# Attention stages with two sets of score banks, unnormalised probabilities and a shorter mask

## The reference

```
# windowed attention of the first block: 8 query heads, 2 key-value heads, head width 64
s_loc = where(|k_pos - q_pos| <= 128, q @ k.T / 8, -inf)      # keys of the tile and its two neighbours
s_ctx = q @ k_ctx.T / 8                                       # all 256 context keys
p = softmax(concat[s_loc, s_ctx, sink_of_head])[..., :-1]     # the sink is one more logit
o = p_loc @ v_loc + p_ctx @ v_ctx

# layers 0 and 1: all keys, no sink
grouped query:  o = softmax(q @ k.T / 8) @ v
differential:   o = (softmax(q1 @ k1.T / 8) - lambda * softmax(q2 @ k2.T / 8)) @ v   # v is 128 wide
```

## Time and profile before

| | |
|---|---|
| median of 3 runs | 4470.28 us (4470.28 to 4470.31) |
| profiled execution | 4471.72 us |
| its span, first to last instruction | 4469.9 us |
| TensorE busy | 3828.3 us |
| window attention | 388.2 to 494.4 us |
| attention of layer 0 | 1564.8 to 1775.9 us |
| attention of layer 1 | 3412.0 to 3579.9 us |

### The profile page before, as it was taken

How to read it: one execution, slowest core, us unless ns; L and a number is a source line. 1 busy time by engine, 2 the same in 40 slices (tenths; PEclk the granted TensorE clock), 3 DMA queues, 4 the chain that set the end, 5 groups by cost and what they waited for, 6 DMA issues and landing times. The chain is left out here.

```text
span 4469.9 us, 46232 instructions
## 1 busy us (share of the span) xinstructions
PE 3828.3 (86%) x18130; PEld 2589.8 (58%) x18130; DVE 1576.6 (35%) x2861; ACT 841.5 (19%) x1725; POOL 1002.0 (22%) x774
## 2 busy tenths in 40 slices
PE   6967967777589778999896999997896889888997
PEld 5865734444365355555453555554784657567886
DVE  3355320000221377334423322334116834334344
ACT  2123220000210155111112100001103511111001
POOL 1300200000023300123231322231142023334442
PEclk8978989899799989999998999998998999999999
DMA  4420289999511100122121223221120012121221
GB/s 187 186 76 15 86 312 396 396 393 400 195 38 57 38 1 1 64 84 87 67 96 38 81 108 113 101 80 46 38 74 16 1 60 82 62 80 60 89 88 48
DMA packets 79670, 496.35 MB, mean 111 GB/s; under 512 B 9568, under 2 KB 10976, under 8 KB 25696
## 3 DMA queue, kind: packets, MB, share of 16 engines
q1 hardware_dynamic: 69808, 469.80, 28.2%
q0 software_dynamic: 3792, 12.85, 0.9%
q10 hardware_dynamic: 5856, 10.75, 0.6%
HBM read 476.58 MB, written 16.78 MB: 110 GB/s over the span
## 5 line engine op out<-in xcount | busy, mean ns | idle before, releaser
L1679 PE MATMUL ps<-expert_weights,experts_x_turned 128*64 128x256 f32 x2112 | 286.3, 432 | 89.5 <-DMA expert_weights<-w_moe 88.0
L1679 PEld LDWEIGHTS ps<-expert_weights,experts_x_turned 128*64 128x64 f32 x2112 | 198.5, 156 | 186.2 <-issue 133.7
L550 PE MATMUL ps<-projected,weight_ring 128*128 128x384 f32 (+1 forms) x672 | 245.8, 521 | 0.0
L550 PEld LDWEIGHTS ps<-projected,weight_ring 128*128 128x128 f32 x672 | 127.7, 190 | 106.1 <-issue 45.9
L1762 DVE TENSOR_TENSOR experts_hidden<-experts_silu_gate,ps 128x256 f32<-128x256 f32 x33 | 13.9, 421 | 495.1 <-PE ps L1679 495.1
L2473 PE MATMUL ps<-h2b,weight_ring 128*128 128x384 f32 (+1 forms) x512 | 153.7, 444 | 23.7 <-PEq L237 23.7
L1977 PE MATMUL ps<-h2b,weight_ring 128*128 128x384 f32 (+1 forms) x512 | 155.1, 447 | 15.4 <-PEq L237 15.4
L814 PE MATMUL ps<-projected 64*128 64x256 f32 (+1 forms) x576 | 120.7, 536 | 54.6 <-ACT attention_prob L877 50.4
L2067 DVE SCALAR_TENSOR_TENSOR projected<-projected,sb_vectors 128x497 f32<-128x497 f32 (+26 forms) x270 | 157.8, 649 | 1.3
L2453 POOL TENSOR_TENSOR mlp_weight_sums<-weight_ring 128x512 f32<-128x512 f32 x32 | 43.6, 1363 | 469.9 <-DMA weight_ring<-w_stream 331.0
L1645 POOL DMA_INDIRECT experts_gathered<-tokens,own_tokens x32 | 28.9, 902 | 521.0 <-PE ps L1667 459.0
(11 more groups left out here) (666 smaller groups left out, 7549.1 us busy)
## 6 DMA issues: line engine op xcount, KB each, us to landing
weight_ring<-w_stream SPq DMA_DIRECT2D x218, 1024.0 KB, 5.0
expert_weights<-w_moe SPq DMA_DIRECT2D x198, 1024.0 KB, 27.6
slot_out<-experts_down_out ACTq DMA_DIRECT2D x66, 128.0 KB, 7.5
weight_ring<-w_stream SPq DMA_DIRECT2D x16, 512.0 KB, 3.7
weight_ring<-w_stream SPq DMA_DIRECT2D x16, 384.0 KB, 3.2
slot_out<-sb_constants SPq DMA_DIRECT2D x15, 256.0 KB, 5.1
sb_x_all<-xT SPq DMA_DIRECT2D x1, 3072.0 KB, 12.1
tokens<-h_tokens ACTq DMA_DIRECT2D x4, 512.0 KB, 4.9
```

What stands on the lines that cost most here:

```text
L550: ins = nc.tensor.matmul(core.ps[:, 2 * slot + half, 0:n], w_of(k), h_of(k)[:, a:a + n], start=(first and k == 0), stop=(last and k == chu ...
L1679: ins = nc.tensor.matmul(out[OWN * j:OWN * (j + 1), :], x_t[:, k, :], w[j][:, k, :], start=(k == 0), stop=(k == KD - 1), skip_group_check= ...
```

## The change

There are four edits.

**Score banks.** Even pairs use banks 0 to 2, odd pairs banks 3 to 5. The two heads lie one behind the other, 768 columns each, so the middle bank holds the end of head 0 and the beginning of head 1. Pieces are cut at bank boundaries: for 768 keys head 0 has 512 + 256 columns and head 1 has 256 + 512. Head 0's piece in the shared bank waits for head 1's. A peak starts when both heads' scores are done, an exponential when both peaks are. The turned probabilities use banks 6 and 7, and the output sum lies in the pair's first score bank, once exponential 0 of the next pair of that parity is done.

**Normalisation.** The exponentials are turned as they are. Their inverse sums are spread over 128 columns by GpSimd (`spread`), turned as one more tile behind the last turn, and copied out with it; VectorE multiplies the output by them when it takes it out of PSUM. For a differential pair VectorE first mixes map 1 into map 0 with the ratio -lambda * sum0 / sum1.

**Order.** The pipeline is one pair deeper: turns are those of p - 2, values those of p - 3, and the first of two turns goes ahead of the scores.

**Mask.** It is added on the two neighbour tiles alone, since the own tile is wholly allowed.

```
+        def scores(p, i):
+            flat = ps[:, 3 * (p % 2):3 * (p % 2) + 3, :].rearrange("p b n -> p (b n)")
+            return flat[:, i * T:(i + 1) * T]
+        flat_t = ps[:, 6:8, :].rearrange("p b n -> p (b n)")
+        def acc(p):
+            return ps[:, 3 * (p % 2), 0:P]
+        def factor(p):
+            b, keys = 2 * (p % 2) + sides[p] - 1, pairs[p]["keys"]
+            return prob_t[:, b, keys:keys + P]
...
             def score(p):
-                if p >= 1:
-                    pe.wait_ge(p_ready, 2 * p)
+                if p >= 2:
+                    pe.wait_ge(p_ready, 2 * p - 2)
+                if p >= 4:
+                    pe.wait_ge(o_out, p - 3)
+                cut = [pieces(i, pr["spans"]) for i in range(2)]
+                for j in range(max(map(len, cut))):
+                    for i in (0, 1) if j == 0 else (1, 0):
+                        if j < len(cut[i]):
+                            (q, k), (at, c, n) = pr["maps"][i], cut[i][j]
+                            if i == 0 and at >= 512:
+                                pe.wait_ge(shared_done, shares[p])
+                            ins = nc.tensor.matmul(scores(p, i)[:, at:at + n], q, k[:, c:c + n], start=True,
+                                                   stop=True, skip_group_check=True)
+                            if i == 1 and j == 0 and pr["keys"] > 512:
+                                ins.then_inc(shared_done, 1)
...
             def transpose(p, i):
-                pe.wait_ge(prob_ready, turn(p, i))
+                if pairs[p]["diff"]:
+                    pe.wait_ge(mixed, mixes[p])
+                else:
+                    pe.wait_ge(p_ready, 2 * p + i + 1)
...
+                if i == sides[p] - 1:
+                    pe.wait_ge(spread_ready, p + 1)
+                    ins = nc.tensor.transpose(flat_t[:, tiles * P:(tiles + 1) * P], spread[:, p % 2, :],
+                                              core.c("ident"))
...
             def values(p):
+                pe.wait_ge(p_ready, 2 * min(p + 2, N - 1) + 1)
...
-            for p in range(N + 2):
+            for p in range(N + 3):
+                if 0 <= p - 2 < N and sides[p - 2] == 2:
+                    transpose(p - 2, 0)
                 if p < N:
                     score(p)
-                if 0 <= p - 1 < N:
-                    transpose(p - 1, 0)
-                if p >= 2:
-                    values(p - 2)
-                if 0 <= p - 1 < N and sides[p - 1] == 2:
-                    transpose(p - 1, 1)
+                if 0 <= p - 2 < N:
+                    transpose(p - 2, sides[p - 2] - 1)
+                if p >= 3:
+                    values(p - 3)
...
         def _(act):
+                    exponential(p - 1, 0)
+                    copy_turned(p - 2, 0)
+                    exponential(p - 1, 1)
+                    copy_turned(p - 2, sides[p - 2] - 1)
...
+        @block.gpsimd
+                nc.gpsimd.tensor_tensor(
+                    spread[:, p % 2, :].rearrange("p (h n) -> p h n", h=n),
+                    core.ones[:, :].rearrange("p (h n) -> p h n", h=n),
+                    inv[:, b:b + n].unsqueeze(2).broadcast_to([P, n, P // n]), ALU.mult).then_inc(spread_ready, 1)
...
         def _(dve):
+            def inverse(p):
+                dve.wait_ge(p_ready, 2 * p + 2)
+                nc.vector.reciprocal(inv[:, b:b + 2], sums[:, b:b + 2]).then_inc(inv_ready, 1)
+                if pairs[p]["diff"]:
+                    nc.vector.tensor_scalar(ratio[:, r:r + 1], inv[:, b + 1:b + 2], sums[:, b:b + 1], neg_lambda,
+                                            ALU.mult, ALU.mult).then_inc(ratio_ready, 1)
+                    nc.vector.scalar_tensor_tensor(prob[:, b, 0:keys], prob[:, b + 1, 0:keys], ratio[:, r:r + 1],
+                                                   prob[:, b, 0:keys], ALU.mult, ALU.add).then_inc(mixed, 1)
+            def scale(p):
+                dve.wait_ge(o_done, turns[p])
+                nc.vector.tensor_tensor(pairs[p]["out"], acc(p), factor(p), ALU.mult).then_inc(o_out, 1)
...
+                    copy_turned(p - 2, 0)
+                    peak(p, 0)
+                    copy_turned(p - 2, 1)
+                    peak(p, 1)
+                    scale(p - 3)
+                    inverse(p - 1)
```

More of the change, by code:

```diff
@@ L753, in _, with attention_phase @@
             add(n - 1)
-def attention_phase(core, name, pairs, mask=None, neg_lambda=None):
+def attention_phase(core, name, pairs, masked=None, neg_lambda=None):
     nc, ps = core.nc, core.ps
-    masked = mask is not None
+    sink = 0 if masked is None else 1
     N = len(pairs)
@@ L766, in attention_phase @@
     turns = np.cumsum(sides).tolist()
-    wide = np.cumsum([n * (pr["keys"] > 512) for n, pr in zip(sides, pairs)]).tolist()
+    split = [not pr["diff"] and pr["keys"] > 512 for pr in pairs]
+    wide = np.cumsum([n * w for n, w in zip(sides, split)]).tolist()
+    shares = np.cumsum([pr["keys"] > 512 for pr in pairs]).tolist()
+    mixes = np.cumsum([pr["diff"] for pr in pairs]).tolist()
     with core.phase(name) as ph:
         prob = ph.sb("prob", [P, 4, T + 8])
-        prob_t = ph.sb("prob_t", [P, 4, T])
+        prob_t = ph.sb("prob_t", [P, 4, T + P])
         shift = ph.sb("shift", [P, 4])
@@ L773, in attention_phase, with turned @@
         inv = ph.sb("inverse", [P, 4])
[L774 to L777, removed]
[L778 to L783 removed]
+        ratio = ph.sb("ratio", [P, 2])
+        spread = ph.sb("spread", [P, 2, P])
+        s_done = [ph.sem(f"scores_done{i}") for i in range(2)]
+        shared_done, peak_ready, p_ready, inv_ready, ratio_ready, mixed, spread_ready, t_done, pt_act, pt_dve, o_done, \
+            o_out = [ph.sem(x) for x in (
+                "shared_bank_done", "peak_ready", "exp_done", "inverse_ready", "ratio_ready", "mixed", "spread_ready",
+                "turned", "pt_scalar", "pt_vector", "out_done", "out_scaled")]
+        block = ph.block()
+        def scores(p, i):
[7 more added lines that the diff above has]
+            return prob_t[:, b, keys:keys + P]
+        def turned(p, i):
+            return pairs[p]["keys"] + (P if i == sides[p] - 1 else 0)
         def turn(p, i):
@@ L789, in wides, with pieces @@
         def wides(p, i):
-            return wide[p] - (sides[p] - i - 1) * (pairs[p]["keys"] > 512)
+            return wide[p] - (sides[p] - i - 1) * split[p]
         def columns(p):
-            return pairs[p]["keys"] + masked
+            return pairs[p]["keys"] + sink
+        def pieces(i, spans):
+            out, at = [], 0
+            for c, n in spans:
+                while n:
+                    m = min(n, 512 - (i * T + at) % 512)
+                    out.append((at, c, m))
+                    at, c, n = at + m, c + m, n - m
+            return out
         @block.sync
@@ new lines, in score @@
+                if p >= 4:
[11 more added lines that the diff above has]
+                                ins.then_inc(shared_done, 1)
+                            if j == len(cut[i]) - 1 and not sink:
+                                ins.then_inc(s_done[i], 1)
@@ new lines, in score @@
+                if sink:
+                    for i in range(2):
+                        for at, c, n in pr["masked"]:
+                            nc.tensor.matmul(scores(p, i)[:, at:at + n], core.c("ident"),
+                                             masked[:, pr["tile"], c - NCTX:c - NCTX + n], start=False,
+                                             stop=True, skip_group_check=True)
+                        keys, row = pr["keys"], pr["sink"] + i
+                        nc.tensor.matmul(scores(p, i)[:, keys:keys + 1], core.ones[0:1, :],
+                                         core.row[0:1, row:row + 1], start=True, stop=True,
+                                         skip_group_check=True).then_inc(s_done[i], 1)
```

115 lines of the change are left out of this document (40 added, 75 removed).

## The result

The kernel after takes **4429.7 us** (median of 4 runs, 4428.44 to 4431.16), the kernel before 4470.3 in the same comparison: a ratio of 0.9909, 95% interval 0.9892 to 0.9926. The forecast was 4429.

What follows compares the result with a forecast made beforehand. TensorE was taken as busiest in attention (485 us), idle 1.11 us per differential pair awaiting exponentials. Gains 22.7 + 3.2 + 10.4 + 4 + 1 - 0.8, rounded to 41, from 4470.3 gave 4429 us, range 4416 to 4440.

Steps and rivals of the forecast that it cites:

- 64 pairs with 768 keys, steady: Attention of both layers: 32 differential pairs gain 0.71 us each (22.7), 32 grouped-query pairs 0.10 each (3.2).
- window stage: 16 window pairs: shorter mask 0.43 us each, fewer waits for exponentials, spread turn adds 0.11; net 0.65 each, 10.4.
- 16 pairs with 256 keys: Layer 0: full-clock period 2.92 to 2.3 us, but no better at 1.2 GHz; gain 0 to 12, taken as 4.
- filling and draining of the two layers: Pipeline ends, counted over three stages: deeper drain costs 4.5 us, freer filling gains 5.5 of 6.6; net 1.
- semaphores to clear: Four more semaphores per stage, cleared by GpSimd ahead of its next stage's first work: at most 0.8 us lost in all.
- I take 1.49 again: Scores of 768-key pairs: passes on both row halves still sum to 1.28 us, so the turn starts after 1.49, as before.
- neighbours end in order: Rival on the scores: a shorter matmul cannot end before a longer one issued ahead; 1.71 instead of 1.28 us, 4458; chance 0.17.
- Differential pairs: 768 keys: output multiply with hand-overs 0.38, scores 1.49, turn 0.82, values 1.50; period 4.19 us against 4.90.
- Grouped-query pairs: 768 keys, TensorE the bound: values 1.46, turn 0.85, scores 1.49, seven-tile turn 0.92; period 4.72 us against 4.82.
- The feared place: Grouped-query pairs: VectorE's copy between the peaks, called tightest; peak, copy, peak end at 4.6 us, values at 4.72.
- GpSimd and the seventh tile: Spread turn adds 0.11 us; GpSimd's multiply, bounded by 0.726, has up to 2 us of cover and costs nothing.
- the bounds that it names: Range of the main case, 4416 to 4440 us: clock 0 to 12, grouped pairs 0.02 to 0.14, filling 0 to 6.

Runs made afterwards that it cites:

- the first experiment: The changed kernel with head 1's 256-column score piece issued ahead of head 0's 512, the rest of the order kept: 4414.6 us, ratio to before 0.9874.

## Why the prediction was right in the sum, and where it was wrong

| term | predicted gain, us | measured, us |
|---|---|---|
| 64 pairs with 768 keys, steady | 22.7 + 3.2 | 8.1 |
| window stage | 10.4 | 11.2 |
| 16 pairs with 256 keys | 4 (0 to 12) | 10.4 |
| filling and draining of the two layers | 1, with the window's | 6.6, what is left of 36.3 |
| semaphores to clear; the rest of the program | -0.8 | 5.2, scatter |

**The step that failed: "I take 1.49 again".** The prediction let head 0's last piece start as soon as the array's half was free and head 1's 256 columns had passed. The half was free, and the columns had passed; the semaphore was not raised. The scores took 1.79 us to the turn instead of 1.49, 0.30 us in each of 64 pairs, 19 us, and the first experiment gave these back (19.1). The semaphore's own time is the missing number: 1.12 us after the group's start, with the piece itself done at 0.70. The rival "neighbours end in order" named the place, but had the mechanism half right and the price too high: by it head 1's 512 would have started 0.43 us late and the pass sum would have been 1.71, 27.5 us. Head 1's 512 started at 0.54, on time; only the piece behind the semaphore was late. By that rule of the Trainium skill (page "TensorE: Matmul & The Clock Gate", section Part 3: matmuls keep program order in start and in end) starts should keep the order too; here head 1's second pass of 256 starts at 0.33, ahead of head 0's second pass at 0.50, although head 0's matmul was issued first. Whether the end itself or only its signal keeps the order can't be told from the trace, since matmul ends are modelled in it. What a waiting engine sees keeps the order, and that is what the rule was worth here.

**Differential pairs.** Turn 0.82 and values 1.50 came as predicted. From the end of the values to the scores it took 0.48, not 0.38: the multiply is 0.29 as taken, but TensorE starts 0.15 us after its end (1643.51 + 0.29 = 1643.80; scores at 1643.95), where 0.05 had been counted. With the scores' 1.79 that makes 4.59. The first experiment's 4.29 is what the prediction's loop was worth without the semaphore; its remaining excess over 4.19 is this hand-over.

**Grouped-query pairs.** Turn of seven tiles 0.91 (taken as 0.92) and values 1.46 held; turn to scores was 0.80, taken as 0.85. With 1.83 for the scores the pair takes 5.00, worse than before. With the score order mended it is 4.67, predicted 4.72. The feared place, VectorE's copy between the peaks, did not bind: TensorE has no idle time on VectorE's account here.

**Window pairs.** 21.48 us for four, predicted 21.9: 0.75 gained per pair, taken as 0.65. The mask gave its 0.42 of them; the waits for the exponentials less the spread turn were worth 0.33, taken as 0.23. The scores come in pieces of 128 to 384 columns here, and only one of 256, as long as itself, is issued ahead of the one that is waited for, whose semaphore comes 0.02 us after its recorded end; the first experiment left the stage at 94.9.

**256 keys and the ends.** The full-clock loop came as predicted (2.3), but the prediction put only 4 us on it because it feared the low clock; the low clock spells shrank instead, here and at the start of layer 1. Even so the greater part here is the loop. Filling gained 7.8 us in layer 1, of which 3.9 is the clock by the experiment that filled it with empty work; the deeper pipeline's drain cost 1.4 us per layer, as predicted 1.5.

**GpSimd and the seventh tile.** 0.40 us, hidden; 0.11 us per pair with 768 keys for its turn, 10 us over the stages with the shorter copies, as the experiment without it shows. The 0.8 us for semaphores can't be told in the time: GpSimd's first instruction behind the attention of either layer comes 1.2 us after the stage's end and came 0.9 after it before, and behind the window stage 1.2 in both.

So the 18 us missing in the steady pairs (25.9 - 8.1) were made up by 6.4 in the pairs with 256 keys, 5.6 in the filling, 0.8 in the window stage and 6 outside, where it is scatter. The forecast fell on the result by compensation. Two slips in its own arithmetic change nothing in this: the bounds that it names give about 4420 to 4442, not 4416 to 4440, and its parts of "faster" sum to 0.89, not 0.88.

## What to carry to other kernels

Where one matmul waits for the semaphore of another on TensorE, issue the matmul that is waited for ahead of any longer one, even of one on the other rows of the array: it was worth 0.3 us per pair here, 19 us, beside the 36 that the whole change brought to attention. When a stage's gain is summed from a steady period, work out the filling of the pipeline and its granted clock as terms of their own, since the filling of one layer (7.8 us) gained as much here as all 64 pairs at their steady pace (8.1). When an idle time is closed by reordering one engine, follow the ring through the other engines first, and check each releaser that a row names against its end: twice the wait only moved, and two instructions that wait for the same event gain nothing by changing places.

## What the runs showed of the hardware

- A matmul's semaphore came when the longer matmul issued ahead of it on the other half of the rows had ended: 0.42 us after its own recorded end with 512 columns ahead (in two orders of what follows), 0.01 to 0.02 with 256 or nothing ahead.
- The halves themselves don't keep a common order of starts: 0.33 for head 1's second pass, 0.50 for head 0's, whose matmul was issued first.
- Empty work on TensorE in the first pairs of layer 1 halved the spell at the low clock (20.5 to 10.2 us). In layer 0, with four transposes added, the first spell fell from 23.9 to 13.7 us, and two of 3.4 us stood in the first pairs with 768 keys.
- Hand-overs: VectorE's multiply to TensorE's scores 0.15 us (their weight load 0.12) after its recorded end, ScalarE's copy to the values' weight load 0.06 to 0.07, TensorE's turn to ScalarE's exponential 0.09.
